# Causal attention on one core: maximum ahead of the inverse, rotary work between the query-key-value tiles, and a feed-forward root that is joined later

## The chip, the cores and the metric

One core of a Trainium2 chip runs the whole kernel in one launch. The metric is the device time in microseconds from start to end of that launch; lower is better. Three runs of the kernel before gave 3621.34, 3627.55 and 3633.1 us, a median of 3627.55.

## What is computed

The reference is two blocks of two layers each, at batch 1 and sequence 512, width 1024, in float32. The change touches mainly the first block, whose layer is (cut to what matters):

```python
def hybrid_layer(x, positions, norm_g, w_in, cmp_pe, cmp_w1, cmp_w2, w_nsa_o, w_sb_o, w_out, w_ff1, w_ff2):
    hn = rms_norm(x, norm_g[0])
    (nsa_q, k_c, v_c, k_s, v_s, k_w, v_w, nsa_g, sb_q, sb_k, sb_v, merge_g) = split_columns(hn @ w_in)
    ...
    q_rope = partial_rope(q_plain, positions).reshape(grp)
    kc = compress_blocks(to_heads(k_c, ...), cmp_pe[0], cmp_w1[0], cmp_w2[0])
    vc = compress_blocks(to_heads(v_c, ...), cmp_pe[1], cmp_w1[1], cmp_w2[1])
    ks = partial_rope(to_heads(k_s, ...), positions)
    kw = partial_rope(to_heads(k_w, ...), positions)
    gates = jax.nn.sigmoid(nsa_g)...
    y_nsa = nsa_attention(q_rope, q_plain, kc, vc, ks, ..., kw, ..., gates) @ w_nsa_o
    y_sb = stick_breaking_attention(...) @ w_sb_o
    ...
    x = x + rms_norm(mixed, norm_g[1])
    hf = rms_norm(x, norm_g[2])
    ff = jnp.square(jax.nn.relu(hf @ w_ff1)) @ w_ff2
    return x + rms_norm(ff, norm_g[3])
```

Rotary turning touches the first 16 of a head's 64 dimensions. Compress adds a table to windows of 32 tokens and puts them through a two-layer net with a gelu. Attention runs over the compressed keys and, with a causal mask, over two sets of full keys, eight heads each. The feed-forward squares a relu, so a positive factor of each token, here the inverse root of its mean square, can be applied to the relu's input or to its output.

## The kernel before

Tokens lie on the free axis: an activation is kept as tiles of 128 features by 512 tokens. Exactness comes from splitting each float32 operand into a high and a low part: ScalarE copies a value into a rounded type (the high part, `split_hi`), VectorE subtracts (the low part, `split_lo`), and TensorE does three products, high by high, low by high and high by low (`mm3`, L159; the three lines L162, L163 and L165 hold nearly all of its time). Weights stream as units of 1 MB through two slots (`load_unit`, `split_hi`, `split_lo`, `unit_ready`, L130 to L156), each unit giving two tiles of output.

Each stage is a `Block`: every engine runs its own instruction list in order and waits on counting semaphores; a stage ends for all engines together. In the first block, a layer runs these stages in turn:

- `stage_qkv` (L480): ten units, 24 tiles. ScalarE takes each tile out of PSUM (`out`, L537) and splits the unit after next; VectorE has only the norm at the start and the low splits.
- `stage_rope` (L573): six matmuls with a turning matrix, products with the cosine on GpSimd and the sine on VectorE, a sum on VectorE; four transposes of values and four of gates; the loads of the compress weights.
- `stage_compress` (L632): VectorE adds the table (L649), TensorE runs 32 matmuls (L661), then the small second layer.
- `stage_cmp_attention` (L701): scores on TensorE (L720), a softmax on VectorE and ScalarE, transposes (L728); beside it, the splits of queries, keys and values for the next stage, the low ones on GpSimd (L812).
- `stage_causal_attention` (L826): 64 steps of 512, 384, 256 and 128 keys. TensorE: scores(i+3), flips(i), values of the unit before (L894). VectorE: reciprocal(i+2), maximum(i+3), low part of step i (L933). GpSimd scales the probabilities by the reciprocal and the gate (L949). ScalarE: high part of step i, exponential(i+3) (L979).
- stick-breaking attention, the merge, and `stage_project` (L1244), which leaves the sum of squares of its output y gathered over features.
- `stage_mlp` (L1294): y is scaled by its root and added to x (`Residual.dve`, `Residual.pool`: VectorE even tiles, GpSimd odd ones), then x is normed (`Norm.pe_all`, `Normed.dve`, `Normed.act`) and split, then eight groups of twelve tiles: four of the first weight (relu on ScalarE, L1450, square, split), eight of the second, which VectorE adds into y (L1519). Beside it run the rows of a modulation table for the second block, on VectorE (`latent_rows`, L1489), ScalarE and GpSimd.
- `stage_residual` (L1536): the same join at the end of the layer.

`keep_busy` (L201) issues fillers, 128x128 matmuls whose result nobody reads. In `pe_spread_columns` (L345) five of them stand ahead of the matmuls that spread an inverse root over the partitions (`pe_rows`, L356). At the end of the kernel one transfer stores the output (L2883).

## Time and profile before

| | us |
|---|---|
| median of three runs | 3627.55 |
| the profiled execution, whole | 3626.38 |
| its span, first to last instruction | 3624.6 |
| TensorE matmul busy (share) | 3434.5 (95%) |
| VectorE busy (share) | 1918.6 (53%) |
| ScalarE busy (share) | 1355.9 (37%) |
| GpSimd busy (share) | 562.1 (16%) |
| mean granted clock of TensorE | 0.980 |

A time in a timeline counts from the span's start. PE is TensorE, PEld its weight loads, DVE VectorE, ACT ScalarE, POOL GpSimd, SP SyncE; "[5.80 <-PE ps L860]" says that the engine was idle for 5.80 us before, and what released it. The granted clock is 1.00 at 2.4 GHz and 0.50 at 1.2 GHz. Matmuls overlap, so their durations don't add up; the distance between starts is what one costs. Names like `w_hi_mix` are tiles; one line can be a helper's, called from many stages.

### The profile page before, as it was taken

How to read it: one execution, taken by the hardware profiler on the slowest of the kernel's cores; microseconds unless marked ns; L12 is line 12 of the kernel's file. 1: busy time of each engine (PE TensorE's matmuls, PEld its weight loads, DVE VectorE, ACT ScalarE, POOL GpSimd, SP SyncE). 2: the span in 40 equal slices, each digit the busy share in tenths (PEclk: the TensorE clock that was granted, in tenths of full speed). 3: DMA queues.
4: the chain of work that ended last, by engine and by line, in shares of the span. 5: the costliest groups of instructions: out<-in, count | busy, mean ns of one | idle time of the engine just before them, and what ended most of it. 6: DMA issues, size and time to landing. Idle time of an engine off the chain costs nothing. (4 is left out here: it accounts for less than half of the span.)

```text
span 3624.6 us, 46448 instructions
## 1 busy us (share of the span) xinstructions
PE 3434.5 (95%) x17926; PEld 2845.7 (79%) x17926; DVE 1918.6 (53%) x2297; ACT 1355.9 (37%) x1991; POOL 562.1 (16%) x394
## 2 busy tenths in 40 slices
PE   7989999999998999999998999899999999999998
PEld 5766878888776687788876888788888788868886
DVE  4264338777525433877765652533333656554444
ACT  4266234444326623444433443312212344432222
POOL 0042003333104200333321110100000100000000
PEclk9999999999899999999999999999999999999999
DMA  3201224443220032344410001112121021112221
GB/s 134 78 1 54 98 105 141 155 153 130 77 96 1 25 115 80 141 162 162 151 53 18 18 12 70 47 60 68 58 69 59 24 71 53 52 36 93 93 97 66
DMA packets 59363, 287.76 MB, mean 79 GB/s; under 512 B 10704, under 2 KB 11984, under 8 KB 31952
## 3 DMA queue, kind: packets, MB, share of 16 engines
q1 hardware_dynamic: 59216, 285.77, 22.7%
q8 instruction: 97, 1.59, 0.2%
q14 instruction: 50, 0.41, 0.0%
HBM read 283.64 MB, written 2.10 MB: 79 GB/s over the span
## 5 line engine op out<-in xcount | busy, mean ns | idle before, releaser
L162 PE MATMUL ps<-h_hi,w_hi_rest 128*128 128x512 f32 (+1 forms) x1072 | 385.1, 359 | 3.0 <-DVE h_lo L396 3.0
L163 PE MATMUL ps<-h_lo,w_hi_rest 128*128 128x512 f32 (+1 forms) x1072 | 363.4, 354 | 0.0
L1353 POOL TENSOR_TENSOR ada_context<-ada_context,ada_scaled 128x768 f32<-128x768 f32 x112 | 287.6, 2568 | 454.6 <-ACT ada_scaled L1437 449.5
L165 PE MATMUL ps<-h_hi,w_lo_rest 128*128 128x512 f32 (+1 forms) x1072 | 321.9, 355 | 0.0
L151 DVE TENSOR_TENSOR w_lo_mix<-w_raw,w_hi_mix 128x2048 fp32r<-128x2048 f32 x94 | 217.2, 2310 | 185.4 <-ACT w_hi_mix L145 185.3
L435 POOL TENSOR_TENSOR x<-x,y 128x512 f32<-128x512 f32 (+1 forms) x32 | 64.5, 2017 | 1516.0 <-DVE y L441 1516.0
L162 PE MATMUL ps<-h_hi,w_hi_mix 128*128 128x512 f32 x736 | 287.0, 390 | 4.5 <-DVE w_lo_mix L151 2.3
L163 PE MATMUL ps<-h_lo,w_hi_mix 128*128 128x512 f32 x736 | 286.5, 389 | 0.0
L165 PE MATMUL ps<-h_hi,w_lo_mix 128*128 128x512 f32 x736 | 286.4, 389 | 0.0
L1519 DVE TENSOR_TENSOR y<-ps,y 128x512 f32<-128x512 f32 (+1 forms) x224 | 165.8, 751 | 219.0 <-PE ps L165 218.4
L145 ACT ACTIVATE w_hi_rest<-w_raw 128x2048 fp32r<-128x2048 f32 x81 | 154.5, 1909 | 326.7 <-PE ps L165 315.4
L162 PE MATMUL ps<-hid_hi,w_hi_rest 128*128 128x512 f32 (+1 forms) x768 | 273.2, 356 | 0.0
L163 PE MATMUL ps<-hid_lo,w_hi_rest 128*128 128x512 f32 (+1 forms) x768 | 260.6, 354 | 0.0
L1450 ACT ACTIVATE sq<-ps 128x512 f32<-128x512 f32 (+1 forms) x128 | 83.4, 651 | 473.0 <-PE ps L165 473.0
L162 PEld LDWEIGHTS ps<-h_hi,w_hi_rest 128*128 128x128 f32 x1072 | 201.3, 188 | 51.6 <-DVE h_lo L396 5.8
L151 DVE TENSOR_TENSOR w_lo_rest<-w_raw,w_hi_rest 128x2048 fp32r<-128x2048 f32 (+1 forms) x85 | 197.5, 2324 | 80.4 <-ACT w_hi_rest L145 80.2
L145 ACT ACTIVATE w_hi_mix<-w_raw 128x2048 fp32r<-128x2048 f32 x92 | 175.4, 1907 | 148.8 <-PE ps L165 134.0
L165 PE MATMUL ps<-hid_hi,w_lo_rest 128*128 128x512 f32 (+1 forms) x768 | 231.0, 355 | 0.0
L1493 DVE SCALAR_TENSOR_TENSOR ada_latent<-ada_raw,cvec,ada_latent 128x768 f32<-128x768 f32 x112 | 225.4, 2013 | 0.0
L163 PEld LDWEIGHTS ps<-h_lo,w_hi_rest 128*128 128x128 f32 x1072 | 201.4, 188 | 29.8 <-issue 1.0
L162 PE MATMUL ps<-hid_hi,w_hi_mix 128*128 128x512 f32 x512 | 205.8, 402 | 0.1
L163 PE MATMUL ps<-hid_lo,w_hi_mix 128*128 128x512 f32 x512 | 200.3, 391 | 0.0
(399 smaller groups left out, 7690.8 us busy)
## 6 DMA issues: line engine op xcount, KB each, us to landing
w_raw<-in_stream SPq DMA_DIRECT2D x205, 1024.0 KB, 4.9
ada_raw<-in_ada_w SPq DMA_DIRECT2D x128, 384.0 KB, 5.2
cmp_w<-in_cmp_w SPq DMA_DIRECT2D x8, 1024.0 KB, 7.0
mla_raw<-in_stream SPq DMA_DIRECT2D x8, 512.0 KB, 3.6
x<-in_x SPq DMA_DIRECT2D x1, 2048.0 KB, 8.7
out<-x SPq DMA_DIRECT2D x1, 2048.0 KB, 7.3
x<-in_ctx SPq DMA_DIRECT2D x1, 1024.0 KB, 11.0
consts<-in_consts SPq DMA_DIRECT2D x1, 768.0 KB, 11.7
```

What stands on the lines that cost most here:

```text
L145: act.activation(k.whi[:, n % 2, 0:width], k.raw[:, n % 2, 0:width], ACT.Copy).then_inc(k.w_hi, 1)
L151: dve.tensor_tensor(k.wlo[:, n % 2, 0:width], k.raw[:, n % 2, 0:width], k.whi[:, n % 2, 0:width].bitcast(F32), ALU.subtract).then_inc(k.w_ ...
L162: pe.matmul(out, whi, xhi, start=start, stop=False)
L163: pe.matmul(out, whi, xlo, start=False, stop=False)
L165: last = pe.matmul(out, wlo, xhi, start=False, stop=stop)
L435: e.tensor_tensor(self.x[:, t, 0:n.tok], self.x[:, t, 0:n.tok], n.src[:, t, 0:n.tok], ALU.add).then_inc(sem, 1)
L1353: pool.tensor_tensor(ada.context, ada.context, ada.scaled[:, j % 2, :], ALU.add).then_inc(m["context"], 1)
L1450: act.activation(k.sqt[:, j % 2, 0:tok], k.ps[:, base:base + tok], ACT.Relu).then_inc(s["relu"], 1)
L1493: dve.scalar_tensor_tensor(ada.latent, ada.raw[j], k.cv[:, j, 0:1], ada.latent, ALU.mult, ALU.add).then_inc(m["latent"], 1)
L1519: dve.tensor_tensor(y[:, j, 0:tok], src, y[:, j, 0:tok], ALU.add).then_inc(s["added"], 1)
```

## The change

It has six parts.

1. `stage_rope` is gone. Its matmuls and transposes are issued by TensorE between the query-key-value tiles (`between(j)`: one turning matmul ahead of each of tiles 7 to 12, the transposes of values ahead of tile 13, of gates ahead of tile 14), the rotations by VectorE between the low splits, the cosine products by GpSimd from the stage's start on, the sigmoid and the copies by ScalarE. VectorE also adds compress's table there. The transfers of the compress weights move into SyncE's list of this stage, two of them into the raw weight slots and two into the first split slots.
2. The splits of queries, keys and values move from `stage_cmp_attention` to `stage_compress`, the low ones from GpSimd to VectorE.
3. In causal attention VectorE issues the maximum of step i+3 ahead of the reciprocal of step i+2.
4. In the first block's feed-forward the first weight is applied to x times the gain, without the root. The root's column sums and rows stand inside the third tile's matmuls, a copy of the rows is kept, and relu becomes one VectorE operation, max(psum, 0) times the rows; both squares go to ScalarE. x's low parts and the gathered squares are made inside the residual join. The projection splits one unit more.
5. `pe_spread_columns` issues two fillers in place of five.
6. The last residual stage stores each tile when it is final, with eight transfers.

```diff
     def pe_spread_columns(self, pe):
-        keep_busy(pe, self.k, 5 * self.pause, self.free)
+        keep_busy(pe, self.k, 2 * self.pause, self.free)
         self.pe_rows(pe)
...
-    def dve(self, dve):
+    def dve(self, dve, behind=None):
         n = self.norm
-        for t in range(n.kt):
-            for c0, w, scale in self.parts:
+        for t in range(n.kt + 2 if behind else n.kt):
+            if behind and t >= 2:
+                behind(t - 2)
+            for c0, w, scale in self.parts if t < n.kt else ():
                 dve.scalar_tensor_tensor(n.src[:, t, c0:c0 + w], n.src[:, t, c0:c0 + w], scale[:, t:t + 1],
                                          n.rb[:, c0:c0 + w], ALU.mult, ALU.mult).then_inc(self.scaled, 1)
-            if t % 2:
+            if t % 2 and t < n.kt:
                 self.add(dve, t - 1, self.even)
...
+            for c in range(2):
+                for r in range(2 if c == 0 else 1):
+                    sp.dma_start(b.w2[:, c, :, 64 * r:64 * r + 64],
+                                 b.w2_src[c].rearrange("(h p) n -> p h n", p=P)).then_inc(b.small_loaded, 16)
+                sp.dma_start(b.pe[:, c, :], b.pe_src[c]).then_inc(b.small_loaded, 16)
+            for u in range(2):
+                sp.wait_ge(k.w_lo, n0 + UNITS_QKV - 1 + u)
+                sp.dma_start(b.cw[u], b.cw_src[u]).then_inc(b.cw_loaded[u], 16)
+            sp.wait_ge(ready, tiles - QT)
+            for u in range(2, 4):
+                sp.dma_start(b.cw[u], b.cw_src[u]).then_inc(b.cw_loaded[u], 16)
...
+            def between(j):
+
+                i = j - ROPE_TILE
+                if 0 <= i < len(srcs):
+                    pe.wait_ge(taken, stored[i])
+                    if i >= 2:
+                        pe.wait_ge(half2, i - 1)
+                    pe.matmul(rope_psum(i), k.c["rope_perm"], srcs[i], start=True, stop=True).then_inc(turned, 1)
+                elif j == V_TILE:
+                    for t in range(QT):
+                        pe.transpose(k.ps[:, 3584 + t * P:3584 + (t + 1) * P], b.vv[:, t * P:(t + 1) * P],
+                                     k.c["ident"]).then_inc(flipped, 1)
+                elif j == GATE_TILE:
+                    pe.wait_ge(gated, 1)
+                    pe.wait_ge(half2, len(srcs))
+                    for t in range(QT):
+                        pe.transpose(k.ps[:, 2048 + t * 24:2048 + (t + 1) * 24], b.gate_t[0:24, t * P:(t + 1) * P],
+                                     k.c["ident"][0:24, 0:24]).then_inc(flipped, 1)
...
-            for u in range(2, UNITS_QKV):
+
+            def rotate(i):
+                dve.wait_ge(turned, i + 1)
+                if i:
+                    dve.wait_ge(rotated, i)
+                dve.tensor_tensor(k.acc[:, 0:SEQ], rope_psum(i), b.sin, ALU.mult).then_inc(half2, 1)
+                dve.wait_ge(half2, i + 1)
+                dve.wait_ge(half1, i + 1)
+                dve.tensor_tensor(dsts[i], k.acc[:, 0:SEQ], k.sqt[:, i % 2, 0:SEQ], ALU.add).then_inc(rotated, 1)
+
+            for u in range(2, 5):
                 split_lo(dve, k, n0 + u)
+            rotate(0)
+            split_lo(dve, k, n0 + 5)
+            rotate(1)
+            rotate(2)
+            split_lo(dve, k, n0 + 6)
+            rotate(3)
+            rotate(4)
+            split_lo(dve, k, n0 + 7)
+            rotate(5)
+            split_lo(dve, k, n0 + 8)
+            dve.wait_ge(b.small_loaded, 80)
+            dve.wait_ge(taken, 5)
+            half = CMP_T // 4
+            for c in range(2):
+                view = b.kv_cmp[:, c, :].rearrange("p (c r) -> p r c", r=CMP_S)
+                for h in range(2):
+                    dve.tensor_tensor(b.blk[:, c, h * half:(h + 1) * half, 0:NC],
+                                      view[:, 0:CMP_S:2, h:h + NC],
+                                      b.pe[:, c, h * half:(h + 1) * half].unsqueeze(2).to_broadcast([P, half, NC]),
+                                      ALU.add)
+            split_lo(dve, k, n0 + 9)
+
+        @block.gpsimd
+        def _(pool):
+            pool.wait_ge(normed.lo_done, KT)
+            for i, src in enumerate(srcs):
+                pool.wait_ge(taken, stored[i])
+                if i >= 2:
+                    pool.wait_ge(rotated, i - 1)
+                pool.tensor_tensor(k.sqt[:, i % 2, 0:SEQ], src, b.cos, ALU.mult).then_inc(half1, 1)
...
+                if j == GATE_TILE - 3:
+                    act.wait_ge(taken, 8)
+                    act.activation(b.gate_t[0:24, :], b.gate_t[0:24, :], ACT.Sigmoid).then_inc(gated, 1)
+                elif j == V_TILE + 1:
+                    act.wait_ge(flipped, QT)
+                    act.activation(b.v[:, :, :].rearrange("p a b -> p (a b)"), k.ps[:, 3584:4096], ACT.Copy)
+                elif j == GATE_TILE + 1:
+                    act.wait_ge(flipped, 2 * QT)
+                    act.activation(b.gate[:, :, :].rearrange("p a b -> p (a b)"), k.ps[:, 2048:2048 + 96], ACT.Copy)
...
-def stage_rope(nc, k, b):
...
+            for br in range(2):
+                dve.wait_ge(k_hi, br + 1)
+                dve.scalar_tensor_tensor(b.ks_lo[:, br, :], b.kr[:, br, :], K_SCALE, b.ks_hi[:, br, :].bitcast(F32),
+                                         ALU.mult, ALU.subtract)
+            dve.wait_ge(v_hi, 1)
+            dve.tensor_tensor(b.vlo, b.v, b.vhi.bitcast(F32), ALU.subtract)
+            for h in range(HEADS):
+                own, other = head_rows(h)
+                dve.wait_ge(q_hi, h + 1)
+                dve.tensor_tensor(b.qs[other, h, :], b.qr[own, h // 2, :], b.qs[own, h, :].bitcast(F32), ALU.subtract)
...
             invert(0)
             invert(1)
             for i in range(STEPS):
+                if i + AHEAD < STEPS:
+                    top(i + AHEAD)
                 if i + 2 < STEPS:
                     invert(i + 2)
-                if i + AHEAD < STEPS:
-                    top(i + AHEAD)
                 low(i)
...
+            if behind:
+                unit_ready(pe, k, n0)
+                keep_busy(pe, k, 6, 6)
+                outs = [tile_out(k, j, tok)[1] for j in range(2)]
+                w = [unit_tiles(k, n0, 0, KT, 256, j) for j in range(2)]
+                for i in range(KT):
+                    pe.wait_ge(raw_lo, i + 1)
+                    for j in range(2):
+                        last = mm3(pe, outs[j], *w[j][i], [(k.hhi[:, i, 0:tok], k.hlo[:, i, 0:tok])], i == 0, i == KT - 1)
+                        if i == KT - 1:
+                            last.then_inc(s["ready"], 1)
...
+                    if first and behind and j == 2:
+                        w = unit_tiles(k, n, 0, KT, 256, 0)
+                        dense_tile(pe, k, outs, w, k.hhi, k.hlo, tok, None, range(0, 3))
+                        n_pre.pe_column_sums(pe)
+                        dense_tile(pe, k, outs, w, k.hhi, k.hlo, tok, None, range(3, 5))
+                        n_pre.pe_rows(pe)
+                        last = dense_tile(pe, k, outs, w, k.hhi, k.hlo, tok, None, range(5, KT))
...
+            if behind:
+                for t in range(KT):
+                    res.wait(act, t)
+                    act.activation(k.hhi[:, t, 0:tok], k.x[:, t, 0:tok], ACT.Copy, scale=gains[:, t:t + 1]).then_inc(raw_hi, 1)
+                    n_pre.act_square_behind(act, t)
+                n_pre.act_root_columns(act)
+                act.wait_ge(n_pre.spread, 1)
+                act.activation(root_rows, n_pre.rb, ACT.Copy).then_inc(rows_done, 1)
...
+                    if behind:
+                        act.wait_ge(s["relu"], T1 * it + j + 1)
+                        if j >= 2:
+                            act.wait_ge(s["hid_lo"], T1 * it + j - 1)
+                        act.activation(squares[j % 2][:, 0:tok], k.sqt[:, j % 2, 0:tok], ACT.Square).then_inc(s["squared"], 1)
+                        hidden_hi(j)
...
+                def weights_lo(half):
+                    c = slice(half * UNIT // 2, (half + 1) * UNIT // 2)
+                    return dve.tensor_tensor(k.wlo[:, (n0 + 1) % 2, c], k.raw[:, (n0 + 1) % 2, c],
+                                             k.whi[:, (n0 + 1) % 2, c].bitcast(F32), ALU.subtract)
+
+                def raw_rest(t):
+                    dve.wait_ge(raw_hi, t + 1)
+                    dve.scalar_tensor_tensor(k.hlo[:, t, 0:tok], k.x[:, t, 0:tok], gains[:, t:t + 1],
+                                             k.hhi[:, t, 0:tok].bitcast(F32), ALU.mult, ALU.subtract).then_inc(raw_lo, 1)
+                    if t:
+                        n_pre.dve_gather(dve, t - 1)
+
+                dve.wait_ge(k.w_hi, n0 + 2)
+                weights_lo(0)
+                n_post.dve_inverse(dve, k.root_cols)
+                weights_lo(1).then_inc(k.w_lo, 1)
+                dve.wait_ge(n_post.spread, 1)
+                res.dve(dve, raw_rest)
+                n_pre.dve_gather(dve, KT - 1)
+                n_pre.dve_inverse(dve, k.root_cols)
+                dve.wait_ge(rows_done, 1)
...
+                    if behind:
+                        dve.wait_ge(s["ready"], (T1 + T2) * it + j + 1)
+                        base, _ = tile_out(k, j % ring, tok)
+                        dve.scalar_tensor_tensor(relu, k.ps[:, base:base + tok], 0.0, root_rows, ALU.max,
+                                                 ALU.mult).then_inc(s["relu"], 1)
+                        if j < T1 - 1:
+                            latent_rows(it, j)
...
+            def _(sp):
+                for t in range(KT):
+                    res.wait(sp, t)
+                    sp.dma_start(store[:, t, :], k.x[:, t, 0:SEQ]).then_inc(stored, 16)
+                sp.wait_ge(stored, 16 * KT)
```

## Rows read from the trace of the kernel before

**Rows 1.** Windows: span, us, busy (instructions) by engine, clock, DMA share, GB/s
```profile
34.70:149.30 114.60, 114.37 (x586) 98.52 (x586) 29.38 (x25) 37.01 (x47) 0.00 (x0) 0.97 0.22 74
149.30:163.10 13.80, 6.18 (x20) 3.02 (x20) 10.89 (x14) 3.63 (x6) 7.57 (x6) 0.89 0.86 318
163.10:181.20 18.10, 17.30 (x76) 8.64 (x76) 1.45 (x4) 2.17 (x7) 0.00 (x0) 0.89 0.01 3
...
199.50:296.20 96.70, 88.32 (x560) 68.18 (x560) 67.15 (x201) 65.07 (x201) 39.32 (x65) 0.98 0.00 1
527.90:560.90 33.00, 29.81 (x141) 21.53 (x141) 23.38 (x32) 11.63 (x20) 7.74 (x4) 0.95 0.43 160
560.90:596.60 35.70, 35.66 (x169) 29.62 (x168) 32.09 (x26) 16.68 (x19) 18.75 (x7) 1.00 0.49 173
```

**Rows 2.** Timeline of TensorE, 149.3 to 200: start, us, what, idle before
```profile
150.02 3.67 PE L597 MATMUL ps<-q,consts 128*128 128x512 f32 x8 [0.73 <-PEq L488]
...
163.17 15.86 PE L661 MATMUL ps<-cmp_w,blk 128*31 128x256 f32 x64 [6.97 <-DVE blk L649]
```

**Rows 3.** Causal stage: waits (total us, times, longest), then TensorE's timeline
```profile
DVE sst L913 <- ACT p L960: 16.2, 41, 0.4
...
241.14 0.33 PE L858 MATMUL ps<-k_hi,q_split 128*128 128x128 f32 x1
...
242.21 0.66 PE L870 MATMUL ps<-consts,p 128*128 128x128 f32 x4 [0.51 <-POOL p L949]
...
243.41 0.39 PE L858 MATMUL ps<-k_hi,q_split 128*128 128x512 f32 x1
...
247.69 0.22 PE L858 MATMUL ps<-k_hi,q_split 128*128 128x128 f32 x1
...
249.12 0.40 PE L858 MATMUL ps<-k_hi,q_split 128*128 128x512 f32 x1
```

**Rows 4.** Timeline of VectorE, 149.3 to 200
```profile
151.88 1.24 DVE L621 TENSOR_TENSOR qr<-acc,sq 128x512 f32<-128x512 f32 x1
...
161.53 0.69 DVE L621 TENSOR_TENSOR kr<-acc,sq 128x512 f32<-128x512 f32 x1
...
190.05 1.66 DVE L774 TENSOR_TENSOR pc<-pc,cst 128x496 f32<-128x496 f32 x1
```

**Rows 5.** Feed-forward: timelines of VectorE, GpSimd, TensorE; ScalarE's group by line
```profile
532.23 1.41 DVE L441 SCALAR_TENSOR_TENSOR y<-y,norm_g,ps 128x512 f32<-128x512 f32 x2 [3.39 <-PE ps L359]
...
565.48 2.29 DVE L151 TENSOR_TENSOR w_lo_mix<-w_raw,w_hi_mix 128x2048 fp32r<-128x2048 f32 x1 [1.05 <-ACT w_hi_mix L145]
...
533.71 1.66 POOL L435 TENSOR_TENSOR x<-x,y 128x512 f32<-128x512 f32 x1 [191.82 <-DVE y L441]
...
560.88 0.39 PE L162 MATMUL ps<-h_hi,w_hi_mix 128*128 128x512 f32 x1
...
L1442 ACT ACTIVATE hid_hi<-sq 128x512 fp32r<-128x512 f32 (+1 forms) x128 | 87.9, 687 | 4.1
```

**Rows 6.** End of the kernel: SyncE's timeline, then GB/s in 40 slices of 3600 to 3625
```profile
3616.91 0.66 SPq L2883 DMA_DIRECT2D out<-x  x1
...
GB/s 0 0 0 0 0 0 0 0 0 0 0 0 0 0 0 0 0 0 0 0 0 0 0 0 0 0 0 0 0 318 383 380 390 387 377 393 387 341 0 0
```

**Rows 7.** Windows about the clock, columns as in rows 1
```profile
163.00:166.00 3.00, 2.83 (x7) 1.24 (x8) 1.55 (x4) 0.79 (x1) 0.00 (x0) 0.50 0.03 14
...
201.00:208.00 7.00, 4.56 (x30) 3.56 (x30) 4.49 (x14) 4.89 (x16) 3.16 (x5) 1.00 0.01 4
208.00:211.00 3.00, 3.00 (x11) 2.13 (x10) 2.37 (x8) 2.08 (x8) 1.66 (x3) 0.50 0.00 0
```

**Rows 8.** A later feed-forward group: timelines of VectorE and of TensorE
```profile
680.89 2.00 DVE L1493 SCALAR_TENSOR_TENSOR ada_latent<-ada_raw,cvec,ada_latent 128x768 f32<-128x768 f32 x1
...
683.71 0.28 PE L1372 MATMUL ps<-consts,ada_latent 128*128 128x1 f32 x2
```

**Rows 9.** Fillers ahead of a root's rows: timeline of TensorE, 924.8 to 946
```profile
928.75 2.47 PE L204 MATMUL ps<-consts 128*128 128x128 f32 x10 [0.32 <-PEq L1323]
```

More of the change, by code:

```diff
@@ L632, in stage_compress, with head_rows @@
-def stage_compress(nc, k, b):
-    added, hidden, gelu, turned, copied, outs_ready = (
-        k.sem(f"cmp_{s}") for s in ("pe_added", "hidden", "gelu", "turned", "copied", "out"))
-    half = CMP_T // 4
-    with nc.Block() as block:
-        @block.vector
-        def _(dve):
-            dve.wait_ge(b.small_loaded, 80)
-            for c in range(2):
-                view = b.kv_cmp[:, c, :].rearrange("p (c r) -> p r c", r=CMP_S)
-                for h in range(2):
-                    dve.tensor_tensor(b.blk[:, c, h * half:(h + 1) * half, 0:NC],
-                                      view[:, 0:CMP_S:2, h:h + NC],
-                                      b.pe[:, c, h * half:(h + 1) * half].unsqueeze(2).to_broadcast([P, half, NC]),
-                                      ALU.add).then_inc(added, 1)
+def stage_compress(nc, k, b):
+    hidden, gelu, turned, copied, outs_ready = (
+        k.sem(f"cmp_{s}") for s in ("hidden", "gelu", "turned", "copied", "out"))
+    q_hi, k_hi, v_hi = (k.sem(f"cmp_{s}") for s in ("q_hi", "k_hi", "v_hi"))
+    K_SCALE = HD ** -0.5
+    def head_rows(h):
+        own, other = slice(64 * (h % 2), 64 * (h % 2) + 64), slice(64 - 64 * (h % 2), P - 64 * (h % 2))
+        return own, other
+    with nc.Block() as block:
@@ L1321, in stage_mlp @@
     squares = (k.acc, k.diag)
+    behind = root_rows is not None
+    if behind:
+        gains = pre[0][2]
+        raw_hi, raw_lo, rows_done = k.sem(f"{name}_raw_hi"), k.sem(f"{name}_raw_lo"), k.sem(f"{name}_root_rows")
     with nc.Block() as block:
@@ L1509, in group @@
                         split_lo(dve, k, n0 + j // 2 + 2, it=it, per=4)
-                    if ada:
+                    if ada and not (behind and j < T1 - 1):
                         latent_rows(it, j)
@@ L1543, in _ @@
                 prefetch(sp)
+        if store is not None:
+            stored = k.sem(f"{name}_stored")
+            @block.sync
+            def _(sp):
[3 more added lines that the diff above has]
+                sp.wait_ge(stored, 16 * KT)
         @block.tensor
@@ L2877, in build @@
         second_block(nc, k, a, second)
-        stored = sem("stored")
-        with nc.Block() as block:
-            @block.sync
-            def _(sp):
-                sp.dma_start(a["out"], k.x[:, :, 0:SEQ]).then_inc(stored, 16)
-                sp.wait_ge(stored, 16)
 def feature_major(t):
```

181 lines of the change are left out of this document (63 added, 118 removed).

## The prediction, made before the change was run

> **What bounds the kernel now.** I read the page's busy table first: TensorE is busy for 95% of the span, so work taken from another engine counts only where TensorE waits for it. Then the windows. In the query-key-value stage TensorE is busy for 114.37 of 114.60 us while VectorE has work for 29.38: what is put on VectorE there is hidden, what is put on TensorE is paid. The rotary stage behind it lasts 13.80 us with 6.18 us of TensorE work; the compress stage has 17.30 of 18.10, at a mean granted clock of 0.89; the causal stage 88.32 of 96.70; the lead-in of the feed-forward, from the end of the projection to its third tile, 29.81 of 33.00 [rows 1]. All of them come twice, for there are two layers. The timeline says who is waited for: TensorE stands for 6.97 us before its first compress matmul, behind VectorE's rotations [rows 2]; in the causal stage VectorE waits 41 times, 16.2 us in all, for ScalarE's exponentials ahead of its reciprocals [rows 3].
>
> The sum is made against the profiled execution, 3626.4 us, which is 1.2 us under the median of the runs shown.
>
> **Rotary stage into the query-key-value stage.** Gone are the 13.80 us from the last dense matmul to the first of compress [rows 1]. Coming back are the same matmuls and transposes between the tiles, 6.18 us of a busy TensorE [rows 1], and one change of block, 0.73 us [rows 2]. Net 13.8 - 6.2 - 0.7 = 6.9 us a layer. Costed at nothing: six rotations (two operations each, 0.69 us, the second up to 1.24 [rows 4]) and compress's four additions, in 85 us of VectorE's idle time. What they could delay is the low split of a weight unit, 2.29 us [rows 5] of the 11 that a unit lasts (114.6 us for ten); a pair of rotations, 3.9 us, still leaves 5. If that cover went, the tile behind would wait the difference. The six cosine products go to GpSimd, idle there; the sigmoid and the copies to ScalarE, with 77 us free. The transfers move too: SyncE issues two of the compress weights after the last units' splits and the other two when the last unit begins, 11 us before the stage ends. 2 MB at the 390 GB/s of the store [rows 6] take 5.4 us; uncovered, those 5 us would stand before compress.
>
> Behind it the clock: in the first 3 us of compress, after the gap, the granted clock was 0.50, the level of 1.2 GHz [rows 7]. The mean of 0.89 over 18.1 us [rows 1] is 4.0 us at that level, 2.0 of them lost. Without the gap they come back; I take 1.6, as the fall needn't be as long each time.
>
> The splits of queries, keys and values go from GpSimd, ScalarE and VectorE in the compressed attention to the compress stage, where VectorE and ScalarE are each free for 16 of 18 us [rows 1]. In the compressed attention an operation with two SBUF operands took 1.66 us while GpSimd worked, and a like one 0.69 us when it did not [rows 4]; that one and a shorter delay of the kind stand in the chain before TensorE's transposes. 1.0 + 0.5 = 1.5 us a layer, at least 0, at most 3.
>
> **Causal attention.** VectorE's order is reciprocal(i+2), maximum(i+3), and the reciprocal waits for an exponential that itself needed the maximum before: a ring through ScalarE. With the maximum first the exponential comes 0.4 us earlier (16.2 / 41 [rows 3]), while a reciprocal can come one maximum, 0.5 us, later, if the maximum waits for its scores; GpSimd's scaling and TensorE's flips hang on it. What is late next is TensorE. The same iteration of its loop takes 249.12 - 247.69 = 1.43 us when fed and 243.41 - 241.14 = 2.27 us when its flips wait for GpSimd [rows 3]: 0.84 us a head, eight heads, 6.7 us a layer at most, and nothing at least. I take 5, nearer the upper end, since the ring is shortened twice in each such wait's unit; the stage's first and last head don't share in it.
>
> **The feed-forward root.** Before, TensorE's third tile starts at 560.88 [rows 5]. After, the first two don't await the root. VectorE interleaves, per tile of x, a scaling (0.66: 1.41 for two, less their overlap), half an addition, the low part and a gathered square, each 0.6 to 0.7 [rows 4, 5], 2.2 us. But GpSimd adds the odd tiles, and its addition, 1.66 us with its own wait, shuts out VectorE's two-operand work for the last 1.2, as in the rotary stage [rows 4, 5]: once in two tiles, so 2.8 us per tile. From the first scaling, at 531.8, the two tiles are done near 554.1, 6.8 us earlier. Then it gives back. Column sums and rows stand inside the third tile, 1.8 us of TensorE. VectorE can start the first group only when the root's rows are copied, 6 us after those tiles: relu, ScalarE's two squares of 0.69, a low part of 0.7, twice, then a split of 2.29 [rows 5]. The split that the fifth tile needs is 2.2 us late, the third low part another 2.1, the eighth latent row 1.5: 5.8 us of waits, against 0.5 before. Net 6.8 - 1.8 - 5.3 = -0.3: nothing gained.
>
> The clock leans on it too. TensorE has 1.36 us of work in each 2.8 us of this phase. At the start of the causal stage it was busy for 4.56 of 7.00 us at 2.4 GHz and was granted 0.50 in the 3 us that followed [rows 7]. If that happens here, the last step and the third tile are slower by 3 us a layer; I take 1.7. The Trainium skill (TensorE: Matmul & The Clock Gate, Part 1: The HAM clock gate) ties the fall to an idle stretch, and this phase has only short ones; by that rule the fall stays out and the sum would be 3.4 us lower. So this part costs 2 x (0.3 + 1.7) = 4 us, between -12 (no shut-out, half the waits) and +12 us.
>
> In the later groups relu goes to VectorE and both squares to ScalarE. VectorE waits 1.3 us for them and comes 0.9 us later to its latent rows, the eighth of which ended at 682.89 against 683.71, when TensorE wanted it [rows 8]: the cover is 0.8 us. I put down 1.5 us for all fourteen groups; at least 0; the upper end is the rival below.
>
> **Fillers and the store.** Of the five fillers ahead of a root's rows three go, at five joins besides the feed-forward's. At half clock their ten passes took 2.47 us [rows 9], so six save 1.5, of which the reciprocal leaves 1.3 (three places); at full clock 0.5 and 0.7: 5.1 us, at least 2 if the clock falls for want of them. The last store was issued at 3616.91 and the program ended at 3624.6; 2.10 MB at 390 GB/s are 5.4 of these 7.7 us, so 2.3 are fixed [rows 6]. By tiles, the last 256 KB take 0.7 + 2.3 from about 3616.7: 3619.7, 4.9 us earlier.
>
> **Sum.** 2 x (6.9 + 1.6 + 1.5 + 5.0) = 30.0, fillers 5.1, store 4.9: 40.0 off; feed-forward 4.0 + 1.5 on. 3626.4 - 34.5 = 3592 us.
>
> **The rivals.**
> Causal attention is unmoved: the wait for ScalarE becomes one of the same length for TensorE's scores, since the maximum now stands ahead of the reciprocal. For it: TensorE is busy for 91% of the stage. Against: its waits are for GpSimd, behind the reciprocal [rows 3]. 3592 + 10 = 3602. Chance 0.2.
> The feed-forward lead-in pays: GpSimd's additions fall beside VectorE's PSUM reads, and the chain of the first group is mostly covered. For it: 6.8 us are there to be had. Against: the shut-out [rows 4]. 6 us a layer less: 3580. Chance 0.15.
> A rotation stalls the dense tiles, so that this stage isn't hidden as the change says: VectorE's wait for a cosine product holds up a weight split behind it. It decides once the wait passes 5 us; 8 us a layer: 3608. Against: GpSimd has nothing else. Chance 0.06.
> Slower than before: every feed-forward group waits. VectorE works for 32.09 of 35.70 us in the first group [rows 1], and with relu on VectorE between latent rows of 2.00 us [rows 8] the low parts come late. It decides from 2.2 us a group (35 / 16 groups); at 3 us it gives 3592 + 48 = 3640. Against: the chain grows by 0.9 us and the cover is 0.8. Chance 0.04.
>
> **How the numbers follow.** The forecast has 0.55. What a measurement of this kernel can tell from no change is 0.3%, 11 us; all cases but the last end below 3616, and the forecast's own tail reaches past it with 0.04. The range, 3574 to 3608, reaches down past the feed-forward case with the full causal bound and up to no causal gain with the clock's loss, leaving out 2 in 10. Faster 0.92, same 0.04, slower 0.04.
>
> **What would show it.** Right: less than 1 us from the last dense matmul to the first compress matmul; a query-key-value stage longer by 6.2 us; compress at clock 1.00; a causal stage of some 91.7 us whose flips hardly wait for GpSimd; the third feed-forward tile near 554, followed by some 4 us of waits for the low weight split and the low part of the hidden tile; the end 3 us behind the last addition. Wrong: a causal stage over 95 us, a TensorE that waits for VectorE in the groups after the first, or a lead-in with its first group (68.7 us before, from 527.9 to 596.6 [rows 1]) that is shorter by over 3 us.

## The result and the profile after

The changed kernel takes 3602.47 us (median of four runs, 3602.30 to 3602.62), the kernel before, beside it, 3625.66 (four runs, 3621.34 to 3633.10). The ratio is 0.9941, with a 95% interval of 0.9924 to 0.9959. The forecast was 3592. The profiled execution has a span of 3600.8 us against 3624.6: 23.8 us less, where the sum said 34.5. (That execution of the kernel before was a long one: in the four later sets of runs its median was 3621.5 to 3623.0 us, which puts the change at 20 us. One later run of that kernel, 5528.7 us at a mean clock of 0.576, is left out everywhere.)

The head of the page of the changed kernel, busy time by engine, and the group of the first weight's matmuls (busy, mean ns, idle before and its releaser):

```profile
PE 3417.6 (95%) x17790; PEld 2834.9 (79%) x17790; DVE 1881.0 (52%) x2313; ACT 1354.1 (38%) x1993; POOL 537.2 (15%) x376
...
L162 PE MATMUL ps<-h_hi,w_hi_mix 128*128 128x512 f32 x736 | 290.0, 394 | 14.7 <-DVE h_lo L1544 12.4
```

and the same group before:

```profile
L162 PE MATMUL ps<-h_hi,w_hi_mix 128*128 128x512 f32 x736 | 287.0, 390 | 4.5 <-DVE w_lo_mix L151 2.3
```

TensorE's share is unchanged. Of the 14.7 us of idle time, 12.4 are waits for VectorE's low parts (`h_lo`), where the whole group had 4.5 before: the first feed-forward tiles now wait while x is being joined. Windows of the changed kernel for the stages of [rows 1], in the same columns: query-key-value, compress, causal attention, and the two halves of the feed-forward's start:

```profile
34.10:155.80 121.70, 120.80 (x606) 101.33 (x607) 39.38 (x41) 39.91 (x53) 7.68 (x6) 0.98 0.30 106
155.80:172.00 16.20, 15.41 (x77) 8.06 (x77) 7.39 (x11) 9.78 (x21) 0.00 (x0) 1.00 0.00 0
189.50:284.70 95.20, 88.47 (x560) 69.17 (x560) 67.35 (x201) 64.75 (x201) 39.61 (x65) 0.98 0.01 1
515.60:543.00 27.40, 20.66 (x80) 16.31 (x81) 20.82 (x30) 11.13 (x18) 6.63 (x4) 0.81 0.51 192
543.00:580.90 37.90, 35.12 (x151) 28.19 (x150) 27.49 (x24) 17.83 (x21) 17.97 (x7) 0.91 0.37 130
```

The rotary stage of 13.8 us is gone and its work stands in the first row. Compress runs at clock 1.00, where it had 0.89. The causal stage is only 1.5 us shorter. The lead-in of the feed-forward, counted from the first column sum of the projection's root, has 27.4 us in place of 33.9. Its first group has 37.9 us up to the table's first rows in place of 30.3 at full clock (the row of it in [rows 1] ends 5.4 us later, behind those rows). TensorE's timeline from the last dense matmul to compress, which answers to [rows 2]:

```profile
154.81 0.28 PE L165 MATMUL ps<-w_hi_qkv,h_lo 128*128 128x256 f32 x1
155.81 1.45 PE L688 MATMUL ps<-cmp_w,blk 128*31 128x256 f32 x6 [0.73 <-PEq L501]
```

The granted clock in one run isn't the granted clock in the next, and it moves more time than most parts of this change. So I measured the parts by distances on TensorE between the same two matmuls of the profiled executions, first layer / second layer, in us:

```
from ... to                                  before          after           forecast of the step
first dense matmul to compress           125.77 / 124.79  119.07 / 119.14   -6.9 each
compress to the causal scores             36.54 / 35.76    33.88 / 33.88    -3.1 each
causal scores to stick-breaking           96.73 / 95.37    95.19 / 94.62    -5.0 each
root of the projection to first rows      64.18 / 63.28    65.28 / 63.95    +2.0 each
first rows to last rows of the table     324.55 / 324.52  325.35 / 325.44   +0.75 each
last rows to the next dense matmul        41.89 / 35.53    38.34 / 40.28    fillers
second block, to its last root               1736.48          1733.83       fillers
last root to the end                          20.51            14.39        -4.9 and -0.7
```

Against the sum, the causal stage falls short by 7.7 us, the fillers by 3.1, the compress and compressed attention stages by 1.7, the query-key-value stage by 1.4; the feed-forward's start cost 2.2 less than said, and the stores at the end gave 0.6 more. The rest is under 1 us.

### The profile page after: what moved, and what is told of

It is laid out like the page before. It is cut to its first block and busy times, and to the rows that moved or that the text cites. A ratio compares the mean times of both kernels' runs of the same rounds, so it can differ in the third digit from the quotient of the medians.

```text
span 3600.8 us, 46138 instructions
## 1 busy us (share of the span) xinstructions
PE 3417.6 (95%) x17790; PEld 2834.9 (79%) x17790; DVE 1881.0 (52%) x2313; ACT 1354.1 (38%) x1993; POOL 537.2 (15%) x376
## 5 line engine op out<-in xcount | busy, mean ns | idle before, releaser
L162 PE MATMUL ps<-h_hi,w_hi_mix 128*128 128x512 f32 x736 | 290.0, 394 | 14.7 <-DVE h_lo L1544 12.4
L1569 DVE SCALAR_TENSOR_TENSOR ada_latent<-ada_raw,cvec,ada_latent 128x768 f32<-128x768 f32 x112 | 216.0, 1928 | 0.0
L165 PE MATMUL ps<-hid_hi,w_lo_mix 128*128 128x512 f32 x512 | 201.1, 393 | 0.0
```

The source lines that it names most:

```text
L162: pe.matmul(out, whi, xhi, start=start, stop=False)
L165: last = pe.matmul(out, wlo, xhi, start=False, stop=stop)
L1569: dve.scalar_tensor_tensor(ada.latent, ada.raw[j], k.cv[:, j, 0:1], ada.latent, ALU.mult, ALU.add).then_inc(m["latent"], 1)
```

## The experiments

All times are medians, beside runs of the kernel before on the same chip in the same minutes: 3622.0 us in the set of the first four kernels, 3621.5 for the next four, 3621.6 for three and 3623.0 for the last.

**The maximum first, alone.** The kernel before with the two statements turned:

```diff
-                if i + 2 < STEPS:
-                    invert(i + 2)
                 if i + AHEAD < STEPS:
                     top(i + AHEAD)
+                if i + 2 < STEPS:
+                    invert(i + 2)
                 low(i)
```

> The kernel before with only the maximum of step i+3 ahead of the reciprocal of step i+2 in causal attention. Theory A (the forecast's 5 us a layer is there, and the other parts of the change hide it): the causal stage falls from 97.1 and 95.7 us (first score matmul to first matmul of the next stage) to about 92 and 91, the run by about 10 us. Theory B (a head lost only the one wait of 0.51 us for GpSimd before, and has two of 0.18 after): 0.13 us a head, the stages come out at 95.5 and 94.9 as in the changed kernel, the run 2.4 us shorter, which a span of 3624.6 would make 3622.

Measured: stages of 95.31 and 94.58 us (to the first matmul of the next stage; the text above counts to its second line, 0.4 more), so theory B: 1.4 and 0.8 us. But the run took 3634.3 us (twelve runs, 3625.1 to 3640.7), 0.27% more than before (0.15 to 0.39%). The traces put this at places that the edit doesn't touch: the first dense matmul starts 3.5 us later, ahead of any attention; the first layer's compress and compressed attention take 39.9 us for 36.5, at a mean clock of 0.71 for 0.76; and the second layer's way from the last rows to the next dense matmul takes 40.7 us for 35.5, at 0.83 for 1.00. The mean granted clock of the twelve runs was 0.979, of before's sixteen 0.982. Why these twelve got less clock isn't shown.

**Five fillers again.** The changed kernel with 5 in place of 2 in `pe_spread_columns`.

> The changed kernel with five fillers again ahead of each spread root in place of two. By the forecast's sum these fillers cost 5.1 us: 3602.5 becomes 3607.6. Theory B (the missing fillers let TensorE's granted clock fall inside the two joins behind the feed-forward, and this pays back most of what they save): the granted clock stays at 1.00 from 915 to 922 us, no loss there, and the run comes out between 3602 and 3605. In either case the other joins, where the clock does not fall, show 0.7 us more each.

Measured: 3602.36 us (3599.2 to 3608.2). Between the medians the three fillers that were taken out make no difference; with five runs that spread over 9 us, a few us either way can't be excluded. Where the clock stays up they cost 0.6 us a join (14.95 for 14.39 us at the end); the mean clock is 0.983 with them and 0.981 without. Theory B asked for a clock that stays up at the first layer's last rows when the fillers are back. It didn't: the granted clock was 0.50 from 906.3 to 916.5 us there, with all five of them.

**The feed-forward part undone.** The changed kernel with

```diff
-        n = stage_project(nc, k, "wo", stream, n, b.mhi, b.mlo, y, SEQ, UNITS_1, wo_norm, 1, beyond=True)
+        n = stage_project(nc, k, "wo", stream, n, b.mhi, b.mlo, y, SEQ, UNITS_1, wo_norm, 1)
...
-                      ... UNITS_1, ff_norm, wo_norm, ada, root_rows)
+                      ... UNITS_1, ff_norm, wo_norm, ada)
```

> The changed kernel with the feed-forward of before in the first block: root joined ahead of the first weight, relu on ScalarE, no unit split beyond in the projection. By the forecast this part costs 4.0 + 1.5 us, so without it 3602.5 - 5.5 = 3597. By the stage times of the two traces (lead-in and first group 1.1 and 0.7 us longer, the wait ahead of the last group's rows 1.1 instead of 0.5 us) it costs 3 us: 3599.5; if the fall of the granted clock in the second layer's last rows (some 5 us with the join) is this part's doing, 3595. A rival: the part gains and is hidden by a clock that fell by chance: 3602.5 or more.

Measured: 3594.34 us (3592.8 to 3597.9), 8 us less than the changed kernel. The start of the feed-forward takes 62.68 and 62.00 us in place of 65.28 and 63.95, the way to the last rows 324.53 in place of 325.35 and 325.44: 6.3 us in all belong to this part, and it is a loss. The clock moves these starts too, but the two sorts don't meet: with two fillers they take 63.4 to 65.6 us in the kernels with this part and 62.0 to 63.0 in those without. (The kernel before has 1.4 us more at the start than this one: its five fillers.)

**ScalarE's order turned as well.** The changed kernel with `exps(i + AHEAD)` ahead of `high(i)`.

> The changed kernel with ScalarE's order in causal attention turned too: exponential of step i+3 ahead of the high part of step i. If TensorE's two waits a head for GpSimd hang on the exponential that stands behind a high part, they shrink or go: up to 0.7 us a head, 11 us over 16 heads, likely 3 to 6, so 3597 to 3600. If they hang on the order of VectorE's low part and maximum instead, the high and then the low part come later and the flips wait for them: the stages stay at 95 us or get longer by up to 3 us each, 3602 to 3608.

Measured: 3670.1 us; the causal stages take 133.5 and 131.2 us. Waits of its first causal stage (engine and line, whom it waited for, total us, times, longest):

```profile
ACT p L972 <- DVE sst L920: 60.2, 61, 1.9
DVE pt_lo L932 <- ACT pt_hi L981: 59.6, 62, 2.0
...
PE ps L882 <- POOL p L961: 27.7, 27, 1.8
```

ScalarE waits for VectorE's maximum in nearly every step, and VectorE for ScalarE's high part. The maximum of step i+3 stands behind the low part of step i-1 on VectorE, that low part needs high part i-1, and this now stands behind exponential i+2: one closed ring with a step of work on each engine in turn. The stage's mean clock is 0.90, so a part of the loss may be the clock's, but TensorE is busy for only 102.3 of its 133.4 us. Order on one engine can lengthen a stage by 38 us; the order that was there had the slack, and turning it further gave none.

**The maximum undone.** The changed kernel with the old order in that place.

> The changed kernel with the order of before in causal attention (reciprocal ahead of maximum), all else as changed. Theory B (the swap is worth one shorter wait a head): both causal stages are 1.4 and 0.8 us longer (96.6 and 95.4 us), 2 us in all, the run some 3605. Theory A (5 us a layer): 10 us more, 3612. A third: with the maximum first, TensorE's many small waits let its granted clock fall more often, as the kernel before with the maximum first alone ran 10 us longer at a mean clock of 0.979 where before had 0.982: then this one is no slower than 3602, at a higher mean clock.

Measured: 3603.94 us (3602.0 to 3607.8), stages of 95.71 and 95.43 us against 95.19 and 94.62. Undoing the swap so costs 0.5 and 0.8 us. The second is theory B's; the first is not its 1.4. What the swap is worth is seen best where the clock is 1.00 from end to end: the old order then takes 95.4 us (four stages of this kernel, the one before and the next one, 95.37 to 95.43), the new one 94.5 to 94.6 (ten stages), which is 0.8 us a layer. In the first layers of four kernels the stage's mean clock is 0.98, and it takes 96.7 and 95.7 us in the old order and 95.2 and 95.3 in the new. This kernel's mean clock of 0.981 is the changed kernel's, so the third guess has nothing for it here.

**The rotary part alone.** The changed kernel with the maximum, the feed-forward, the fillers and the store undone.

> The kernel before with the rotary stage inside the query-key-value stage and the splits in the compress stage, and no other part of the change (old order of the maximum, old feed-forward, five fillers, one store). Forecast: 2 x (6.9 + 1.6 + 1.5) = 20 us under before, 3602 to 3606 against 3622. By the stage times of the two traces it is 2 x 8.4 = 17 us, 3605, and the stages from the query-key-value matmuls to the causal scores come out as in the changed kernel (119, 16.2, 17.7 us). If a rotation held up dense tiles, the first of these would be longer than 119.

Measured: 3609.32 us (3606.1 to 3616.7), 12 us under before. By the stages it is more: the query-key-value stage takes 119.13 and 118.31 us, compress and the compressed attention 33.87 and 33.94, 17.6 us less in the four together. The profiled executions differ by 16.8 us (spans of 3607.8 and 3624.6), the medians by less, since that one of before lies 5 us above its median here. No rotation holds up a dense tile: 119.1 is 125.8 less 6.7.

**GpSimd's product left out.** The changed kernel without normalization and gates of causal attention:

```diff
-                pe.wait_ge(s["scaled"], i + 1)
+                pe.wait_ge(s["expd"], i + 1)
...
-        @block.gpsimd
-        def _(pool):
...
```

> The changed kernel without GpSimd's multiplication of the probabilities by reciprocal and gate; TensorE's flips wait for the exponential alone (the output so lacks normalization and gates). It shows what of the causal stage hangs on reciprocal and GpSimd. If these two are the last link (theory A's picture), TensorE is fed throughout: a head takes 10.5 us in place of 11.1, the stages 91 us, the run 8 us less. If the ring of ScalarE's high part, VectorE's low part and maximum and ScalarE's exponential sets the pace, waits for the high and low part take their place: 93 to 95 us.

Measured: 3587.29 us, stages of 87.89 and 87.88. The window of the first one, in the columns of [rows 1]:

```profile
190.40:278.20 87.80, 83.96 (x560) 66.86 (x560) 67.03 (x201) 63.96 (x202) 0.31 (x1) 1.00 0.00 1
```

So 7 us a layer hang on the path from an exponential through the reciprocal and GpSimd to the flips. The rest of the ring doesn't take their place. Nor is it that VectorE works faster with GpSimd idle: it is busy for 67.03 us, and for 67.35 in the changed kernel.

**Values ahead of the flips.** The changed kernel without the feed-forward part, and in TensorE's loop:

```diff
-                flips(i)
                 if i >= QT + 1:
                     values((i - QT - 1) // QT, (i - QT - 1) % QT)
+                flips(i)
```

> The changed kernel without its feed-forward part, and with TensorE's value matmuls ahead of the flips in each step of causal attention. The flips are then asked for 0.5 to 1.2 us later in a step, more than the 0.18 us that they wait: if only their place is wrong, the waits go, 0.3 to 0.7 us a head, 5 to 10 us in all, 3594 less that: 3584 to 3589. If the ring around the engines sets the pace, the later flips push everything behind them back: 3594 or longer, up to 3640.

Measured: 3590.87 us (3584.3 to 3594.0), stages of 93.53 and 93.50 us, 1.1 less than without the edit (94.61 and 94.58, there at a mean clock of 1.00, here at 0.98). TensorE's waits for GpSimd fall to 1.8 us, but it now waits 1.5 us for VectorE's low part. A late operand isn't cured by asking for it later within the same step.

**One step more ahead.** The changed kernel without the feed-forward part, and

```diff
-    P_RING, ST_RING, AHEAD = 6, 8, 3
+    P_RING, ST_RING, AHEAD = 6, 8, 4
...
             invert(1)
+            invert(2)
...
-                if i + 2 < STEPS:
-                    invert(i + 2)
+                if i + 3 < STEPS:
+                    invert(i + 3)
```

> The changed kernel without its feed-forward part, and with scores, maximum, exponential and reciprocal of causal attention one step further ahead of the flips (four and three steps in place of three and two). Without GpSimd's product in the chain a stage took 87.9 us. Theory C (the path exponential, reciprocal, GpSimd has two steps of lead, 2.6 us, and needs a little more at the wide steps): the stages fall from 94.6 to 88 to 90 us, 10 to 13 us in both, 3594 becomes 3581 to 3584. Theory D (the ring of high part, low part, maximum and exponential limits it): that ring has a step more too, but the same order on each engine, and the stages stay at 93 to 95 us; where scores then wait for an exponential, longer than 95.

Measured: 3583.75 us (3581.3 to 3587.3), a ratio of 0.9891 to before (0.9876 to 0.9905); the stages take 88.67 and 88.77 us. The window of the first, and TensorE's wait for GpSimd in it:

```profile
191.90:280.50 88.60, 84.48 (x560) 66.87 (x560) 65.97 (x201) 64.30 (x201) 39.47 (x65) 1.00 0.01 1
```

```profile
PE ps L882 <- POOL p L962: 0.5, 1, 0.5
```

Theory C. VectorE, ScalarE and GpSimd are busy for about as long as they were; the one wait for GpSimd that is left is the first step's. Four operations were moved ahead at once, so which of the leads was needed isn't shown by this run alone.

**Twelve fillers in the feed-forward's start.** The changed kernel with

```diff
                         if i == KT - 1:
                             last.then_inc(s["ready"], 1)
+                    if i < KT - 1:
+                        keep_busy(pe, k, 12, 5)
```

> The changed kernel, feed-forward part included, with twelve fillers (0.65 us at full clock) behind each of the first seven steps of the two tiles that await x's low parts. By the forecast the fall of the clock there costs 1.7 us a layer: the granted clock stays at 1.00 from 522 to 540 us and the lead-in with the first group gets 1 to 3 us shorter than 65.3 and 64.0 us, the run 3599. If the fillers stand in the way of work that is ready, it is 0 to 3 us longer a layer; if the clock falls nevertheless, unchanged.

Measured: 3625.99 us, the start 78.14 and 76.78 us. I had the price wrong: a filler is two passes in the trace, so that the ten of [rows 9] are five fillers. TensorE's group of fillers from 522.7 to 549 us, six of the seven times twelve:

```profile
L204 PE MATMUL ps<-consts 128*128 128x128 f32 x144 | 17.3, 277 | 0.0
```

17.3 / 6 = 2.9 us for twelve, where a step had 1.1 to spare. The clock was 0.50 once more, from 522.5 to 525.9 us, and 1.00 from there to 543.

**Four and values.** The two edits of causal attention together.

> As the kernel with four steps ahead, and TensorE's value matmuls ahead of the flips. If one step more already feeds TensorE, this adds nothing (within 0.5 us a stage of that kernel). If the flips still wait for GpSimd there, it takes 1 us a stage more off, as it did alone (94.6 to 93.5 us): 3580 to 3582.

Measured: 3581.77 us (3577.4 to 3585.0), ratio 0.9881 (0.9864 to 0.9899), stages of 89.45 and 89.46 us: 0.7 us longer than with four steps alone. Once TensorE is fed, the later flips only push the rest back. The two runs can't be told apart; either is 0.5% faster than the changed kernel (8 of its 19 to 21 us are the feed-forward part, which both leave out) and 1.1% than the one before.

**Four fillers.** As with twelve, but four (8 passes, 17.3 / 18 = 1.0 us and not the 0.5 of the text).

> The changed kernel, feed-forward part included, with four fillers behind each of those seven steps in place of twelve. Twelve were dearer than expected: the ten of the rows before took 1.24 us at full clock and not 0.54, so twelve take 1.5, and a step has only 1.1 us to spare; the stage with the first group grew by 12.9 us. Four take 0.5 us and fit. If the falls of the clock there (3 us at 525 and 2 at 534) cost time, they go, and the lead-in with the first group gets 0.5 to 2 us shorter than 65.3 and 64.0 us, the run 3600. If each step waits for VectorE's low part anyway, so that the half clock is hidden in the waits, it stays within 0.3 us, and the forecast's 1.7 us a layer was no cost of its own.

Measured: 3604.28 us (3603.1 to 3611.0); the start takes 66.00 and 64.43 us, 0.7 and 0.5 longer. The same window of the changed kernel and of this one, in the columns of [rows 1]:

```profile
525.00:528.00 3.00, 3.00 (x9) 2.33 (x8) 2.21 (x4) 0.72 (x1) 1.66 (x1) 0.50 1.05 425
```

```profile
525.00:528.00 3.00, 3.00 (x21) 2.66 (x20) 2.21 (x5) 0.72 (x1) 1.69 (x1) 1.00 1.05 433
```

The clock is held and nothing is won: each step waits for VectorE's low part anyway, so TensorE catches up at the next wait. The changed kernel's own trace says the same: behind its two falls of the clock in this phase TensorE still waits for a low part, 0.96 us at 531.12 and 0.89 us at 540.15.

## Why the prediction was right, and where it was not

The time lay in the range, 10.5 us above the forecast and on the first rival's 3602. That rival is nearly what happened in the causal stage (2.3 us gained, where it had nothing and the forecast 10), though not by its mechanism. That the whole comes out at its very number is luck: the causal stage fell short by 7.7 us and not by 10, and the misses of the other terms make up the difference.

**Rotary stage.** The steps hold. Compress starts 1.0 us after the last dense matmul, 0.73 of it the change of block. The query-key-value matmuls take 119.1 us where before they and the rotary stage took 125.8 and 124.8: 6.7 and 5.65 for the 6.9. The second layer's stage took 118.0 to 119.4 us in the kernels that share this part, so 1 us there is the clock's and not the change's. No rotation holds up a dense tile in the changed kernel either: from its first dense matmul to the last of this stage TensorE has no idle time of over 0.2 us. Behind it I forecast 3.1 and got 2.7 and 1.9: compress itself gave 1.9 and 1.4, as said, the compressed attention 0.8 and 0.5 of the 1.5. VectorE's operations there were shorter, 0.67 us for 1.24 and 1.66, and TensorE's wait for the last of them in the first layer went from 6.0 to 4.4 us. But VectorE now waits 1.1 us for the second half's scores, where it had waited 0.3.

**Causal attention.** This is the step that failed, and in it only the choice between the bounds. "0.84 us a head, 6.7 us a layer at most" was right: without the product 7 us go, with one step more 6. The prediction's own sign of being wrong, a stage over 95 us, came in the first layer (95.19). What failed is "I take 5, nearer the upper end, since the ring is shortened twice". The swap did remove VectorE's wait for the exponential, and put the wait for the high part in its place. First the waits of the changed kernel in that stage, then TensorE's timeline:

```profile
DVE pt_lo L932 <- ACT pt_hi L981: 19.0, 24, 1.5
...
PE ps L882 <- POOL p L961: 3.6, 16, 0.6
...
DVE sst L925 <- ACT p L972: 0.9, 4, 0.4
```

```profile
218.49 0.33 PE L882 MATMUL ps<-consts,p 128*128 128x128 f32 x1 [0.18 <-POOL p L961]
...
219.80 0.66 PE L882 MATMUL ps<-consts,p 128*128 128x128 f32 x4 [0.18 <-POOL p L961]
```

and from the waits of the kernel before in its causal stage, two rows that I had not weighed:

```profile
DVE pt_lo L920 <- ACT pt_hi L969: 7.2, 16, 1.0
...
PE ps L870 <- POOL p L949: 4.6, 9, 0.5
```

Before, a head had one wait of 0.51 us for GpSimd [rows 3], now it has two shorter ones: nine waits of 4.6 us became sixteen of 3.6 in this stage, and nine of 4.7 became seventeen of 4.3 in stages at a clock of 1.00. VectorE's 16.2 us of waiting for exponentials went down to 0.9, and its waiting for the high part up from 7.2 to 19.0. The wait moved from one statement of VectorE's loop to the next; by my reading, since the same engines are visited in the same order with the same two steps of lead. The rival said that the maximum would wait for its scores; it waits 7.8 us for them in place of 6.6. So the rival's time came by a third way. What pays is distance: one step more of lead for scores, maximum, exponential and reciprocal together gives 5.9 us a layer, with no operation added. That the path through GpSimd is the one that was short of it is what the run without the product adds.

The idle time printed for TensorE understates such a wait: at a clock of 1.00, 4.3 us of it went down to 0.5, and the stage from 94.6 to 88.7 us. In the trace of the changed kernel the flips at 231.04 have 0.18 us of idle time, but start 0.45 us behind the matmul ahead of them, where 0.11 is usual.

**Feed-forward.** "Nothing gained" was right: the way to the first rows is 1.1 and 0.7 us longer than before, for the 0.3 and the clock's 1.7. The third tile comes 27.4 us after the root's sums, where it took 33.9 and 33.0: 6.4 and 5.6 us earlier, fillers included, for the 6.8. VectorE needs 2.5 to 2.6 us a tile where I had 2.8, but not for the reason that I gave. No shut-out by GpSimd's additions is to be seen: from 523 to 541 us no operation of VectorE takes over 0.91 us (a low part takes 0.9 us beside an addition of GpSimd and 0.74 otherwise). What stands between them are waits for ScalarE's high part, such as

```profile
527.50 0.90 DVE L1544 SCALAR_TENSOR_TENSOR h_lo<-x,norm_g,h_hi 128x512 fp32r<-128x512 f32 x1 [0.79 <-ACT h_hi L1469]
```

five of them, of 0.65 to 0.80 us. The term had nearly the right size by the wrong cause. Then the waits that were named, in TensorE's timeline of the changed kernel:

```profile
557.75 0.50 PE L162 MATMUL ps<-hid_hi,w_hi_mix 128*128 128x512 f32 x1 [1.79 <-DVE w_lo_mix L151]
...
560.87 0.79 PE L162 MATMUL ps<-hid_hi,w_hi_mix 128*128 128x512 f32 x1 [0.99 <-DVE hid_lo L1590]
```

for the low split 1.8 of 2.2 us, for the low part 1.0 of 2.1 (1.5 in the second layer). The latent row costs nothing in the first layer and 0.7 us in the second. They are less than forecast, but in the first layer the clock falls among them: 0.50 for 5 us from 560 on.

```profile
560.00:565.00 5.00, 4.13 (x10) 3.26 (x11) 2.68 (x5) 3.86 (x5) 2.03 (x1) 0.50 0.42 177
```

I had put the clock's 1.7 us in the two early tiles. It falls there too, but in this trace costs nothing to speak of: with two falls ahead of it in the first layer and one in the second, the third tile comes after 27.4 us in both. What counts is where the fall comes. With the maximum undone it came at the last step and the third tile in both layers (0.50 from 541.5 to 544.9 us in the first), and with five fillers in the second; there the third tile came after 28.9, 29.0 and 29.4 us, 1.4 to 2.0 later, which is the forecast's 1.7. Back in the changed kernel, in the second layer the clock is 1.00 at the fifth tile and its neighbours (1465 to 1472 us), and the way to the first rows is 1.3 us shorter than in the first, in spite of longer waits. So the term had about the right size, but in these runs it stood in another place, and in one layer of two. By the Trainium skill (TensorE: Matmul & The Clock Gate, Part 1: The HAM clock gate) the clock falls after an idle stretch, and by that rule the fall was to stay out of this phase; the trace disagrees, with waits no longer than 2.0 us in it. The later groups cost 1.7 us for the 1.5, though all of it at one place: each group takes its 46.3 us as before, and only the last group's rows wait, 1.14 us for 0.52.

**Fillers and store.** Sized at 5.1, the fillers gave 2.0 in the two traces and nothing between the medians with five and with two. The number is that of the bound "at least 2 if the clock falls for want of them", but its reason isn't shown: the clock fell at the same rows with five of them. The eight stores gave 5.5 us for the 4.9 (20.49 us from the last root to the end in the kernel with the rotary part alone, 14.95 with five fillers and eight stores): the queue's last transfer is issued at 3598.8, and the end comes 2.4 us after GpSimd's last addition, at 3598.40, not 3. SyncE's row for [rows 6], then GpSimd's last one:

```profile
3591.55 7.21 SPq L1636 DMA_DIRECT2D out<-x  x8
```

```profile
3596.76 1.64 POOL L435 TENSOR_TENSOR x<-x,y 128x512 f32<-128x512 f32 x1 [0.27 <-DVE y L443]
```

## What to carry to other kernels

In a software pipeline over several engines, count for each operand how many steps lie between its making and its use, and lengthen the shortest lead (here 5.9 us of 94.6); turning two statements on one engine moves the wait to the next statement, and the wrong turn closes a ring (133 us for 95). Whether a join should be put off is read from what stands behind it: here it brought two tiles forward by 6 us and gave back 8. And before a part of 1 us is judged by whole runs, look at how much the clock moves them: here the stages said 2 us less where the run said 10 more.

## What the runs showed of the hardware

The granted clock fell after waits far shorter than I had thought needed. In the last rows of the table TensorE waited 0.52 us before and 1.14 us after the change, and was otherwise busy. Windows of the kernel before and of the changed one about that place, columns as in [rows 1]:

```profile
914.00:916.00 2.00, 1.48 (x9) 0.97 (x7) 2.00 (x4) 1.17 (x2) 0.00 (x0) 1.00 0.00 0
916.00:918.00 2.00, 2.00 (x15) 1.87 (x15) 2.00 (x5) 0.73 (x2) 0.00 (x0) 0.98 0.03 8
918.00:920.00 2.00, 2.00 (x9) 1.72 (x8) 1.67 (x3) 1.17 (x2) 0.00 (x0) 0.50 0.00 0
```

```profile
1810.00:1812.00 2.00, 1.18 (x6) 0.64 (x4) 2.00 (x4) 1.17 (x2) 0.00 (x0) 1.00 0.00 0
1812.00:1814.00 2.00, 1.69 (x12) 1.58 (x13) 2.00 (x5) 0.63 (x1) 0.00 (x0) 1.00 0.00 0
1814.00:1816.00 2.00, 2.00 (x12) 1.77 (x11) 2.00 (x4) 0.94 (x2) 0.00 (x0) 0.71 0.00 0
```

What stands there between the dense matmuls are ones of a single column. Before, the fall came in the first layer and not in the second, after in the second and not in the first, with the same instructions in both, and in the kernel with the maximum first alone in both layers. In the kernel before it cost 3 us up to the join. That such falls come and go is also how one kernel's runs spread: before from 3617.9 to 3637.3 us at mean clocks of 0.983 to 0.978. The changed kernel's four runs lie within 0.3 us, and all at 0.980 or 0.981. Which of a kernel's timings makes the fall regular stays open.
